# A hybrid decoder step on one core: the first down weights split on chip, group-1 loads in halves, the last two K blocks interleaved, and the final norm scaled by VectorE

## What is computed

```python
x += W_out [attention || mLSTM](RMSNorm(x))
u = jnp.einsum('btd,df->btf', RMSNorm(x), w_up)             # 1024 -> 4096
x += jnp.einsum('btf,fd->btd', jnp.square(jax.nn.relu(u)), w_down)
y = rms_norm(x, norm_f_g)                                    # x * rsqrt(mean(x*x) + eps) * gain
# and the sample's key and value caches, shifted by 8 rows, are outputs too
```

## Time and profile before

| what | us |
|---|---|
| median of 3 runs (lowest, highest) | 2995.04 (2988.67, 2995.75) |
| the profiled execution, its own time | 2992.78 |
| its span, first to last instruction | 2991.0 |
| TensorE busy | 2737.8 (92%), mean granted clock 0.96 |
| VectorE busy | 1834.0 (61%) |
| ScalarE busy | 1079.5 (36%) |
| GpSimd busy | 651.7 (22%) |
| DMA | 642.33 MB, 215 GB/s on average |

### The profile page before, as it was taken

One profiled execution on the slowest core, in us unless ns is written; L12 is line 12 of the kernel. 1 busy time (PEld: TensorE's weight loads), 2 busy tenths in 40 slices (PEclk: granted clock), 3 DMA queues, 4 the chain that ended last, 5 costly groups with the idle time before them and its releaser, 6 DMA issues. The chain is left out here.

```text
span 2991.0 us, 46001 instructions
## 1 busy us (share of the span) xinstructions
PE 2737.8 (92%) x17331; PEld 2293.8 (77%) x17331; DVE 1834.0 (61%) x3890; ACT 1079.5 (36%) x1984; POOL 651.7 (22%) x539
## 2 busy tenths in 40 slices
PE   7999999999999978999879998888887999899996
PEld 5878788778777766678767886888776888778885
DVE  5522555233788755577566666555554777877776
ACT  4301322111676752423354554544443111321113
POOL 1212012120455440211100001000001344533333
PEclk9999999999999988999989998999999999999998
DMA  4464243444464548957567779576779677776762
GB/s 155 150 233 154 95 139 130 158 131 147 129 203 134 171 157 319 407 205 262 205 229 261 271 267 336 202 251 236 241 246 337 231 248 248 258 271 224 238 234 76
DMA packets 348899, 642.33 MB, mean 215 GB/s; under 512 B 39375, under 2 KB 237139, under 8 KB 328326
## 3 DMA queue, kind: packets, MB, share of 16 engines
q1 hardware_dynamic: 281516, 543.44, 52.6%
q10 hardware_dynamic: 66026, 91.95, 8.5%
q0 software_dynamic: 1152, 4.19, 0.4%
HBM read 461.65 MB, written 244.95 MB: 236 GB/s over the span
## 5 line engine op out<-in xcount | busy, mean ns | idle before, releaser
L2639 PE MATMUL bank<-mlp_h_hi,mlp_wu_hi 128*128 128x272 f32 (+1 forms) x1344 | 448.5, 334 | 83.5 <-ACT mlp_made L3013 47.8
L2640 PE MATMUL bank<-mlp_h_lo,mlp_wu_hi 128*128 128x272 f32 (+1 forms) x1344 | 443.6, 330 | 0.0
L2641 PE MATMUL bank<-mlp_h_hi,mlp_wu_lo 128*128 128x272 f32 (+1 forms) x1344 | 443.2, 330 | 0.0
L3293 DVE TENSOR_TENSOR mlp_acc<-mlp_acc,bank 128x512 f32<-128x512 f32 x440 | 300.2, 684 | 147.3 <-PE bank L2641 140.7
L2639 PE MATMUL bank<-mlp_wd_hi,mlp_u_hi 128*128 128x512 f32 x896 | 353.7, 395 | 36.0 <-DVE mlp_acc L3293 30.3
L2640 PE MATMUL bank<-mlp_wd_lo,mlp_u_hi 128*128 128x512 f32 x896 | 352.9, 394 | 0.0
L2641 PE MATMUL bank<-mlp_wd_hi,mlp_u_lo 128*128 128x512 f32 x896 | 352.6, 393 | 0.0
L2639 PEld LDWEIGHTS bank<-mlp_h_hi,mlp_wu_hi 128*128 128x128 f32 x1344 | 261.6, 195 | 114.5 <-issue 56.7
L3072 ACT ACTIVATE mlp_u_hi<-mlp_u_raw 128x768 fp32r<-128x768 f32 x126 | 113.0, 944 | 471.7 <-POOL mlp_u_raw L2936 471.3
L2640 PEld LDWEIGHTS bank<-mlp_h_lo,mlp_wu_hi 128*128 128x128 f32 x1344 | 261.9, 195 | 20.1
L2641 PEld LDWEIGHTS bank<-mlp_h_hi,mlp_wu_lo 128*128 128x128 f32 x1344 | 261.1, 194 | 20.0
(11 more groups left out here) (391 smaller groups left out, 5468.5 us busy)
## 6 DMA issues: line engine op xcount, KB each, us to landing
mlp_wd_lo<-wd SPq DMA_DIRECT2D x46, 1024.0 KB, 7.6
mlp_wd_hi<-wd SPq DMA_DIRECT2D x45, 1024.0 KB, 5.5
mlp_u_raw<-u SPq DMA_DIRECT2D x256, 128.0 KB, 2.3
out_win_k_sample<-in_cache_k SPq DMA_DIRECT2D x48, 680.0 KB, 7.2
out_win_v_sample<-in_cache_v SPq DMA_DIRECT2D x48, 680.0 KB, 6.4
mlp_wu_raw<-in_w_up SPq DMA_DIRECT2D x30, 1024.0 KB, 7.3
wd<-mlp_un_hi SPq DMA_DIRECT2D x32, 896.0 KB, 4.4
wd<-mlp_un_lo SPq DMA_DIRECT2D x32, 896.0 KB, 7.3
```

The costliest lines, as they stand in the source:

```text
L2639: nc.tensor.matmul(out, ah, bh, start=fresh and k == 0, stop=False, skip_group_check=not fresh)
L2640: nc.tensor.matmul(out, ah, bl, start=False, stop=False, skip_group_check=not fresh)
L2641: ins = nc.tensor.matmul(out, al, bh, start=False, stop=k == n - 1, skip_group_check=not fresh)
L3293: v.tensor_tensor(a, a, b[:], ALU.add).then_inc(summed, 1)
```

## The change

**Transfers.** In `project` SP issues the cache copies more evenly: four more in the first group, two per step in the second, and the nine in a row that stood behind the gate tables are gone; `project_out` has nine copies instead of ten; in the up sets 1 to 6 there are two each. `project_out` loads the four quarters of `h` one per step in steps 11 to 14, not all in step 11, and sums them one step later. Only block 17's split weights are kept; block 16 is loaded raw and split again. At the border the loads come in halves: the columns that are needed first, then the rest.

**Units.** Times are given in half sets: in group 1 a unit begins every third half set. Its load is issued by ScalarE, half a set ahead of the sums; the high part is stored before the low part is made, and the low part is made half a set after the sums.

**First down block.** Its weights are loaded raw in set 46, summed and split in sets 46 and 47, and not read from `K.wd`.

**Down.** The steps of blocks 6 and 7 are interleaved, the sample step comes last in a block, and each block's weights are spread over the steps in which their buffer is free. The gain and the scale are applied by one VectorE operation per tile; GpSimd's `gains` and ScalarE's scaling are gone. GpSimd no longer waits for the gain's load.

```diff
@@ project, project_out
-                    K.copy_cache(sp)
+                    for e in range(g + 1):
+                        K.copy_cache(sp)
...
-                            copies(GN[0] * (b - 2) + 3, 8 if b < 4 else 4)
+                            copies(GN[0] * (b - 2) + 3, 8)
...
                         tables.sync_ends(sp)
-                        copies(40 + 3, 9)
...
-                if 2 <= t < 12:
+                if 2 <= t < 11:
                     K.copy_cache(sp)
-                if t == 11:
+                if 11 <= t < 15:
                     for q in range(2):
                         sp.wait_ge(M.h_out[q], 16 * 4)
-                    for q in (1, 3, 0, 2):
-                        M.load_h(sp, K, (0, 2, 4, 5)[q], q, 0, M.h_in[q])
+                    q = (1, 3, 0, 2)[t - 11]
+                    M.load_h(sp, K, (0, 2, 4, 5)[q], q, 0, M.h_in[q])
...
-                if 12 <= t < 16:
-                    h_sum(t - 12)
+                if 13 <= t < 17:
+                    h_sum(t - 13)
@@ mlp, tables
-    KEPT = (NC, NC + 1)
+    KEPT = (NC + 1,)
-    unit_sets = sorted(list(range(15)) + list(range(18, 45, 2)) + [27, 33, 39])
-    unit_at = {s: w for w, s in enumerate(unit_sets)}
+    EARLY = 15
+    phase = [2 * s for s in range(EARLY)] + [2 * 18 + 3 * w for w in range(UNITS - EARLY)]
+    unit_load = {at: w for w, at in enumerate(phase)}
+    unit_sum = {at + 1: w for w, at in enumerate(phase)}
+    unit_rest = {at + 2: w for w, at in enumerate(phase)}
...
+    ORDER = [(kb, p) for kb in range(6) for p in range(5)]
+    ORDER += [(6, 0), (6, 1), (6, 2), (7, 0), (6, 3), (6, 4), (7, 1), (7, 2), (7, 3), (7, 4)]
@@ mlp, SP
-            if s - 1 in unit_at:
-                store_unit(unit_at[s - 1])
-            if s in unit_at:
-                load_unit(unit_at[s])
+            for ph in (2 * s, 2 * s + 1):
+                if ph in unit_rest:
+                    store_unit(unit_rest[ph], 1)
+                if ph in unit_sum:
+                    store_unit(unit_sum[ph], 0)
+            if s < 13 or 18 <= s < 44:
+                for e in range(2 if 1 <= s < 7 else 1):
+                    K.copy_cache(sp)
...
-                sp.dma_start(wd_hi[0][:].rearrange("p a j c -> p (a j c)").bitcast(F32), K.wd[0, 0]).then_inc(wd_first[0], 16)
+                        sp.dma_start(wd_raw0[:, 0:7:2, j, 256 * e:256 * e + 256], K.ins["w_down"][0, j, e].rearrange("p (a c) -> p a c", a=4))\
+                            .then_inc(wd_first, 16)
@@ mlp, GpSimd
-        pool.wait_ge(gain_f_in, 16)
         for st in steps:
...
-                gains(4 * before.g + before.p)
@@ mlp, ScalarE
+        def load_unit(w):
+            kb, j, e = unit_of(w)
+            if w:
+                act.wait_ge(un_out, 32 * w)
+            act.dma_start(un_raw[:, 0:7:2], K.ins["w_down"][kb, j, e].rearrange("p (a c) -> p a c", a=4)).then_inc(un_in, 16)
...
+            if g == 1 and 2 * s in unit_sum:
+                unit_hi(unit_sum[2 * s])
             if early:
                 w_hi(ci + 1, 0)
+            if 2 * s in unit_load:
+                load_unit(unit_load[2 * s])
+            if early:
                 w_hi(ci + 1, 1)
...
-                A(tile(F, e), tile(F, e), ACT.Copy, scale=fin[:, 7, 2 * F + e:2 * F + e + 1]).then_inc(y_ready, 1)
@@ mlp, VectorE
+        def first_down_low(k):
+            sl = slice(2 * k, min(2 * k + 2, 7))
+            dve.wait_ge(wd_hi_ready, k + 1)
+            v.tensor_tensor(wd_lo[0][:, sl], wd_raw0[:, sl], wd_hi[0][:, sl].bitcast(F32), ALU.subtract).then_inc(wd_lo_ready, 1)
...
+        def final_scale(F, done):
+            dve.wait_ge(f_newton, F + 1)
+            if F == 0:
+                dve.wait_ge(gain_f_in, 16)
+            for e in range(2):
+                a = acc[:, F % 4, 2 * e:2 * e + 2].rearrange("p a c -> p (a c)")
+                v.scalar_tensor_tensor(a, a, fin[:, 7, 2 * F + e:2 * F + e + 1], gain_f[:], ALU.mult, ALU.mult).then_inc(done, 1)
```

More of the change, by code:

```diff
@@ L1745, in __init__ @@
         self.h_in = [sem(f"mlp_h_in{q}") for q in (0, 2, 4, 5)]
+        self.h_late = [sem(f"mlp_h_late{q}") for q in range(5)]
         self.h_mid, self.h_s = sem("mlp_h_mid"), sem("mlp_h_s")
@@ L2711, in mlp @@
     own, pool_own = M.own, sem("mlp_pool_own")
-    wd_first = [sem(f"mlp_wd_first{q}") for q in range(4)]
+    wd_first, wd_t, wd_hi_ready, wd_lo_ready = (sem("mlp_wd_" + n) for n in ("first", "t", "hi", "lo"))
     wd_in = [[sem(f"mlp_wd_in{b}{q}") for q in range(4)] for b in range(2)]
@@ L2718, in mlp @@
     gain_f_in, summed = sem("mlp_gain_f_in"), sem("mlp_summed")
-    f_sum, f_ssq, f_var, f_root, f_newton, f_gained = (sem("mlp_f_" + n) for n in ("sum", "ssq", "var", "root", "newton", "gained"))
+    f_sum, f_ssq, f_var, f_root, f_newton= (sem("mlp_f_" + n) for n in ("sum", "ssq", "var", "root", "newton"))
     y_ready, y_last = sem("mlp_y_ready"), sem("mlp_y_last")
@@ L2736, in mlp @@
-    N = len(steps)
-    ends = steps[-1].mm0 + 7
-    pair = {st.m: st for st in steps if st.p is not None}
-    first_of = {st.kbi: st for st in reversed(steps)}
-    samp = {st.kbi: st for st in steps if st.p is None}
-    M_END = 64
-    def nth(F):
-        return 4 if F is None else F + (F >= 4)
+        for kb, p in ORDER:
+            if g == 0 and p == 4:
+                continue
+            st = Step()
+            st.g, st.kb, st.p, st.kbi, st.n = g, kb, p if p < 4 else None, 8 * g + kb, len(steps)
+            st.m = sum(a.p is not None for a in steps) if p < 4 else None
+            st.before = max((a.n for a in steps if a.g == g and a.p == st.p), default=None)
+            st.mm0 = steps[-1].mm0 + (3 if steps[-1].p is None else 7) if steps else 7 * S0
+            st.po0 = steps[-1].po0 + (3 if steps[-1].p is None else 7) if steps else 0
+            st.F = 4 * g + p if kb == 7 and p < 4 else None
+            steps.append(st)
@@ new lines, in mlp @@
+    pair = {st.m: st for st in steps if st.p is not None}
+    samp = {st.kb: st for st in steps if st.p is None}
+    final = {st.F: st for st in steps if st.F is not None}
+    M_END = len(pair)
+    SAMPLES = 8
+    down_at, samples_at, convert_at = {}, {}, {}
+    for kbi in range(1, 16):
+        users = [st.n for st in steps if st.kbi == kbi]
+        free = max((st.n for st in steps if st.kbi == kbi - 2), default=-1) + 1
+        for q in range(4):
+            down_at.setdefault(free + q * (users[0] - free) // 4, []).append((kbi, q))
@@ L2746, in nth_raw @@
+    for kb in range(8):
+        at = samp[kb - 1].n + 1 if kb else final[2].n
+        samples_at[at], convert_at[at + 1] = kb, kb
     def nth_raw(ci):
-        return ci if ci < NC else ci - len(KEPT)
+        return ci - sum(k < ci for k in KEPT)
     def mm_end(st):
@@ L2774, in piece @@
         return q * n, n
-    kept_out, kept_in = sem("mlp_kept_out"), [sem(f"mlp_kept_in{e}") for e in range(2)]
+    kept_out, kept_in = sem("mlp_kept_out"), sem("mlp_kept_in")
     block = K.ctx_mlp.enter_context(nc.Block(no_gpsimd_drain=True))
@@ L2949, in _ @@
                 sums(st.m + 2)
-            before = steps[st.n - 1] if st.n else None
-            if before and before.kb == 7 and before.p is not None:
-                gains(4 * before.g + before.p)
     @block.scalar
@@ L3049, in _ @@
                 w_hi(ci + 1, 2)
+            if s == LAST:
+                first_down_hi(2)
             squares(s, 1)
+            if s == LAST:
+                first_down_hi(3)
+            if g == 1 and 2 * s + 1 in unit_sum:
+                unit_hi(unit_sum[2 * s + 1])
+            if 2 * s + 1 in unit_load:
+                load_unit(unit_load[2 * s + 1])
             if s == 15:
@@ L3054, in _ @@
                 hi_of(1, 1, 0)
-            if s == LAST:
+            squares(s, 2)
+            if g == 0 and 2 * s + 1 in unit_sum:
+                unit_hi(unit_sum[2 * s + 1])
+            squares(s, 3)
+            if s == LAST - 1:
                 act.wait_ge(u_sums, 4)
@@ L3233, in _ @@
             up_post(s, 1)
+            if g == 1 and s > 16:
+                unit_work(2 * s)
             if s in (16, 17):
@@ L3284, in down_post @@
                 if i == 0:
-                    dve.wait_ge(summed, steps[st.n - (4 if st.g == 0 else 5)].po0 + 7)
+                    dve.wait_ge(summed, steps[st.before].po0 + 7)
             elif i == 2:
@@ L3299, in sample_post @@
             if st.kb:
-                dve.wait_ge(summed, steps[st.n - 5].po0 + 3)
+                dve.wait_ge(summed, steps[st.before].po0 + 3)
             else:
@@ L3308, in final_sums @@
         def final_sums(F):
-            st = pair[28 + F if F < 4 else 60 + F - 4]
-            dve.wait_ge(summed, st.po0 + 7)
+            dve.wait_ge(summed, final[F].po0 + 7)
             a = acc[:, F % 4]
```

273 lines of the change are left out of this document (124 added, 149 removed).

## The result

The changed kernel is slower: 3062.78 us (4 runs, 3060.99 to 3064.46) against 2993.14 (4 runs, 2988.67 to 2995.75), a ratio of 1.0234 with a 95% interval of 1.0216 to 1.0252. Forecast was 2931. The time came out as the rival to which I gave 4 in 100, "slower than before, by the units"; more than half of the loss came by a mechanism that the rival did not have. The profiled execution took 3062.39 with a span of 3060.1, 69.1 more than before.

The account below looks back on a forecast made before the run. TensorE was taken to bound the kernel, so only stretches where it waits or runs below full clock could change. Eight gains summing to 61.7 us, taken from 2992.8, gave 2931; forecast 2910 to 2943 (0.60), 2898 to 2962 leaving out 2 in 10.

Parts of the forecast that it names:

- slower than before, by the units: Rival: ScalarE stops at each unit's load, holding up TensorE; from 23 us a unit, 2993 and above; chance 0.04.
- Units, group 0: Sets 0 to 15: one kept block gains net 3 us, group 0 having slack of several us per set.
- Units, group 1: Sets 17 to 47: chain of units sets the pace, 77 us per six sets; 48 lost against 60, gain 12.
- the four cases: Group 1 units, by load at set's head or middle and q: 3, 0, 6.1 and 8.6 us beyond 14.8 each.
- The bound of that term: Units in group 1: between 40 us gained and 20 lost; loss 80 with both transfer legs 2 us longer.
- Loads of `h`: project_out: slow step returns to 12.87 us, 12.5 gained; last h_sum costs 2.29; net gain 10.2.
- Project: In project, TensorE's gap at 590 to 630 us shrinks without nine copies in a row; gain 5, bounds 0 and 9.
- Border: Between the groups, sets 15 to 17: half loads bring data earlier; gain 8 of 24.8 us lost, bounds 0 and 15.
- Down start: Start of the down products: fewer K.wd reads and no wait for the gain's load; gain 16.5 us.
- Final norm: End of the first down group: interleaved steps lose 14 us against 18.5; gain 4.5.
- my worst case: Down scalings: each of 16 waits 0.72 us for a GpSimd sum on shared ports, 11.5 us added; 2 kept.
- End: After TensorE's last full step: 18.3 us against 18.7, and two stalls fewer bring 2; gain 2.5.

Follow-up runs that it names:

- e1: Changed kernel with group 0's unit high store issued by SP behind the next set's up load, not ahead of it; 3009.0 us.
- e5: e1 with the 26 cache copies of sets 18 to 43 moved into the first down steps; 2973.3 us.
- e3: Changed kernel with the unit's load issued by SP behind the stores of the same half set, instead of by ScalarE; 3044.8 us.
- e11: Kernel before, with project's cache copies spread as in the change and nine copies instead of ten in project_out; 2977.0 us.
- e8: Kernel before, with GpSimd's wait for the gain's load moved to its first multiplication with the gain; 2981.7 us.
- e10: Changed kernel with units as before, 26 copies in down steps, scaling late, and each high store issued once un_hi is ready; 2910.9 us.
- e12: e10 with Newton's operations and the scalings back ahead of a step's third add, as in the change; 2915.3 us.
- e2: Changed kernel with the units at the sets of the kernel before, ScalarE's load and two separate stores kept; 3031.4 us.

## Why the prediction was wrong

By its steps:

- **Units, group 0 (the step that failed).** The prediction gave sets 0 to 15 a gain of 3 us with "slack of several us per set" and took the later up loads at 4 us, in group 1 alone: "Add 4 for up-weight loads that SP now issues later, since it waits for `un_hi` before them". The step named the mechanism and priced it only where the load has a whole set of slack. In group 0 the load is needed in the set in which it is issued. Measured, sets 0 to 15 lost 63.0 us instead, and the edit that undoes this alone (e1) gave 62.3 of them. Had I followed SP's queue for one set of group 0, as I did ScalarE's and VectorE's for group 1, the ring would have been closed on paper: the up load behind `un_hi`, `un_hi` behind the unit's load, that load behind the previous unit's low store, and the low store behind the up load.
- **Units, group 1.** The chain was the right bound, and the four cases in the queues held to the microsecond (21.0 against 21). Wrong were the two legs, taken as 4.9 and 4.5 from transfers "without another in front". The low store's leg is 7.0 on the mean, and from load to sums it is 6.9 where I had 5.7 (4.9, and 8 once); two of the four loads landed only after 7.0 and 7.6. The trace of before had said so: in its sets 17 to 47 a unit's load took 7.6 us by the median and a low store 7.4, while 4.9 was one load's and 4.4 the high store's, the first of each pair. Without the copies (e5) the same four units take 83.9 us, so the copies are a part of it. 91.5 instead of 77 us for six sets, and the windows give 442.2 - 2556 x 0.128 = 115 us lost where I had 48. That (91.5 - 64.4) x 17/4 is also 115 is in part luck, for it leaves out the slack of the first units and the 4 us of set 46.

The row of before for these loads, 1895 to 2277 us (count, KB, median us to landing):

```profile
mlp_un_raw<-in_w_down SPq DMA_DIRECT2D x16, 512.0 KB, 7.6
```

- **The bound of that term.** "With both 2 us longer it is 80" was worked out wrong: 17 units x 4 us are 68, not 32, so the far end of the term was 116 and the range would have reached to 2999. The size that came true was inside the uncertainty that I had named, and the range did not carry it.
- **The slower rival** asked for 23 us per unit; the units took 22.9 on the mean in group 1 and 21.2 to 25.6 in group 0. Its reason, ScalarE's stop, is worth 24 us by e3 and nothing in group 0.
- **Loads of `h`** right in size: 9.8 against 10.2, though e11 leaves open how much of it is the copy that was dropped ahead of them. The last `h_sum` costs 2.3 as said (2.28 in the row below), and the step from 1437 to 1450 runs at 13.0.

```profile
1479.08 2.28 DVE L2549 TENSOR_TENSOR mlp_h_raw<-mlp_h_raw 128x2048 f32<-128x2048 f32 x1
```

- **Project** too small: 12.2 against 5. The stretch that I measured, 590 to 630, was cut too short; the one from 560 to 640 loses 80 - 305 x 0.226 = 11.1, for the clock is low around the idle time and TensorE already stops for 1.4 us ahead of 586. The same window holds 45 matmuls more after the change, 10 us.
- **Border** 4.4 against 8 in the changed kernel, and 4.2 to 9.5 in the kernels where the ring is open, without an order that a run explains.
- **Down start** 14.2 against 16.5 by the window, but some 10 once the 4 us that set 46 now takes longer are counted to it; e8 shows that the gain's wait is about half of what TensorE waited. GpSimd now waits 17.65 us for `u` itself, which was named as what is late next.
- **Final norm** wrong by 6: the end of the first down group loses 21.0, not 14. Product 5 waits for the third add in five steps, up to 5.2 us. Moving the scaling behind that add (e10 against e12) takes back 5.7 of the waiting. What makes up the rest is not shown. VectorE's scalings in the changed kernel's timeline:

```profile
2655.77 2.96 DVE L3372 SCALAR_TENSOR_TENSOR mlp_acc<-mlp_acc,mlp_fin,mlp_gain_f 128x1024 f32<-128x1024 f32 x2
...
2679.70 2.48 DVE L3372 SCALAR_TENSOR_TENSOR mlp_acc<-mlp_acc,mlp_fin,mlp_gain_f 128x1024 f32<-128x1024 f32 x2
```

GpSimd's sum that began at 2657.73, beside the first of these, took 1.59 us, where one alone takes 0.74:

```profile
2657.73 1.59 POOL L2941 TENSOR_TENSOR mlp_u_raw<-mlp_u_raw 128x256 f32<-128x256 f32 x1
...
2660.79 0.74 POOL L2944 TENSOR_TENSOR mlp_u_raw<-mlp_u_raw 128x256 f32<-128x256 f32 x1
```

Three of the eight pairs of scalings ran beside a sum and took 2.96 to 3.02, about 0.5 longer; the other five took 2.48. By the rule of the Trainium skill ("SBUF — State Buffer", "SBUF: two separate sides"), a VectorE operation with two SBUF inputs and a GpSimd one hold their shared ports in turn, so that the later one of two has to wait; the trace agrees. On VectorE that is 1.5 us in all, where my worst case was 11.5 and I had kept 2.
- **End** 4.2 against 2.5, as far as it goes.

**What stays open.** Which terms of the gain outside the units are exact to better than some 8 us, since every stretch was read from one execution of each kernel and equal code differed by that much. Why set 46 takes 4 us longer. How the remaining 14 us of e2 divide between ScalarE's stop and the split stores was not tried alone, nor whether units every three half sets would pay once the chain is as short as in e10.

## What to carry to other kernels

When a wait is added to an in-order queue, follow that queue for a whole period in every phase of the program, and write down each transfer behind the wait with the time at which its data are needed; two engines that each wait for the other's last round make a ring, whose period is the sum of its legs and which no engine's busy share names. Take the duration of a transfer on such a chain from where the same neighbours run, not from the shortest in the trace. And storing each half of a result as soon as it exists is worth something only behind the loads that the next step needs: the same early store cost 62 us of the up sets at one place of SP's queue and gave 19 at another.
